# Tile 0's gates, up and output projections first; tile 1's later, during tile 0's search and first expert rows

## What is computed

```python
sh1, sc1, gt1, sh2, sc2, gt2 = split(silu(c) @ w_cond + b_cond)      # adaLN, 12 blocks of 512 columns
h = layernorm(x) * (1 + sc1) + sh1
q, k, v, gu, gv, ga, gg = split(h @ w_in)                            # 9 blocks of 512 columns
attn = causal attention with ALiBi (8 heads of 64)
sgu = gelu(gu) * (lower triangle of w_spatial @ LN(gelu(gv)) + b)    # 8 groups, chunks of 128 tokens
merged = sigmoid(ga) * (attn @ w_attn_up) + sigmoid(gg) * (sgu @ w_gmlp_up)
x = layernorm(ALPHA * x + (1 + gt1) * (merged @ w_out)) * ln1_g + ln1_b
h = layernorm(x) * (1 + sc2) + sh2
for head in range(8):                                                # PEER: 128 x 128 experts
    s = (h @ w_peer_q[head]) against two tables of 128 keys          # two halves of 128
    e, g = the 16 best sums of one key of each half, softmax over them
    p += sum over the 16 of g * gelu(h . peer_u[e]) * peer_v[e]
out = layernorm(ALPHA * x + (1 + gt2) * p) * ln2_g + ln2_b
```

## Time and profile before

| | |
|---|---|
| median of 3 runs | 966.8 us (965.15 to 969.27) |
| span of the profiled execution | 968.9 us |
| TensorE busy | 804.9 us, 83% |
| VectorE busy | 604.0 us, 62% |
| GpSimd busy | 541.7 us, 56% |
| ScalarE busy | 196.0 us, 20% |
| DMA | 338.30 MB, mean 349 GB/s |

### The profile page before, as it was taken

How to read it: one execution, slowest core, us unless ns; L and a number is a source line. 1 busy time by engine, 2 the same in 40 slices (tenths; PEclk the granted TensorE clock), 3 DMA queues, 4 the chain that set the end, 5 groups by cost and what they waited for, 6 DMA issues and landing times.

```text
span 968.9 us, 8991 instructions
## 1 busy us (share of the span) xinstructions
PE 804.9 (83%) x2516; PEld 451.6 (47%) x2516; DVE 604.0 (62%) x1359; ACT 196.0 (20%) x494; POOL 541.7 (56%) x529
## 2 busy tenths in 40 slices
PE   5999999999768687887979787796979688696884
PEld 5877578778424233433334343343334343343331
DVE  6336585225679756576575848557484856687556
ACT  1012122201122312131221213122121213133111
POOL 1000000000478776777777777777777777777772
PEclk9999999999969888989889897997989798898988
DMA  9998974491799999999999999999999999999994
GB/s 348 373 359 315 342 270 174 176 353 37 243 356 350 339 396 372 357 409 366 380 385 392 409 391 410 408 355 386 380 411 351 409 409 354 405 405 379 410 409 196
DMA packets 112267, 338.30 MB, mean 349 GB/s; under 512 B 9184, under 2 KB 20976, under 8 KB 112112
## 3 DMA queue, kind: packets, MB, share of 16 engines
q0 software_dynamic: 73728, 268.47, 71.8%
q1 hardware_dynamic: 35936, 67.11, 19.5%
q10 hardware_dynamic: 2576, 2.37, 0.8%
HBM read 336.87 MB, written 1.05 MB: 349 GB/s over the span
## 4 chain that ended last, share of the span: by engine, by line
PE 46%; POOL 20%; issue 14%; DMA 8%; DVE 7%; ACT 2%; ACTq 2%; DVEq 0%; POOLq 0%
POOL ring L354 20%; PE bank L1142 20%; PE bank L965 9%; DMA ring<-in_peer_u_dram,small 8%; PE bank L1068 3%; PE bank L1082 3%; PE bank L958 3%; DVE ring L811 2%; PE bank L1105 2%; PE bank L914 1%; ACTq L412 1%; PE bank L931 1%; ACT small L510 1%; PE bank L919 1%; DMA x_sb<-in_x_dram 1%
## 5 line engine op out<-in xcount | busy, mean ns | idle before, releaser
L1142 PE MATMUL bank<-ring,small 128*128 128x512 f32 x1012 | 490.0, 646 | 126.3 <-ACT small L510 125.6
L354 POOL DMA_INDIRECT ring<-in_peer_u_dram,small x256 | 269.5, 1053 | 283.8 <-issue 279.2
L811 DVE CUSTOM_DVE_ANT_0 ring<-ring,h_sb 128x1024 f32<-128x1024 f32 x256 | 310.2, 1224 | 185.6 <-DMA ring<-in_peer_u_dram,small 178.5
L1142 PEld LDWEIGHTS bank<-ring,small 128*128 128x128 f32 x1012 | 207.3, 208 | 399.5 <-issue 314.7
L354 POOL DMA_INDIRECT ring<-in_peer_v_dram,small x256 | 268.2, 1047 | 83.2 <-issue 74.5
L965 PE MATMUL bank<-hT,ring 128*128 128x256 f32 x448 | 102.0, 387 | 1.7 <-ACT hT L405 1.1
L965 PEld LDWEIGHTS bank<-hT,ring 128*128 128x128 f32 x448 | 85.8, 194 | 17.0 <-issue 5.4
L510 ACT ACTIVATE small<-ident,small 128x128 f32<-128x128 f32 x253 | 77.4, 388 | 67.6 <-DVE small L802 66.7
L588 DVE SCALAR_TENSOR_TENSOR ln<-ring,c_col,ln 128x512 f32<-128x512 f32 x77 | 57.9, 752 | 2.7
L1105 PE MATMUL bank<-wpq,hT 128*128 (+1 forms) x240 | 54.2, 379 | 0.0
L505 ACT ACTIVATE small<-small 128x8 f32<-128x8 f32 x32 | 6.7, 208 | 222.7 <-DVE small L811 222.7
(11 more groups left out here) (154 smaller groups left out, 491.5 us busy)
## 6 DMA issues: line engine op xcount, KB each, us to landing
ring<-in_w_cond_dram SPq DMA_DIRECT2D x10, 2048.0 KB, 13.8
ring<-in_w_in_dram SPq DMA_DIRECT2D x8, 2048.0 KB, 12.9
wpq<-in_w_peer_q_dram SPq DMA_DIRECT2D x8, 1024.0 KB, 11.9
ring<-in_w_cond_dram SPq DMA_DIRECT2D x4, 1024.0 KB, 14.5
ring<-in_w_out_dram SPq DMA_DIRECT2D x2, 2048.0 KB, 10.7
ring<-in_peer_u_dram,small POOLq DMA_INDIRECT x256, 6.5
ring<-in_peer_v_dram,small POOLq DMA_INDIRECT x256, 6.4
ring<-in_w_in_dram SPq DMA_DIRECT2D x2, 1024.0 KB, 13.3
```

The source lines that it names most:

```text
L354: nc.gpsimd.indirect_dma_start(out=dst[e], out_offset=None, in_=table[0], in_offset=bass.IndirectOffsetOnAxis(ap=idx[:, k:k + 1], axis=0)) ...
L811: V.tensor_tensor_reduce(u_ring[e], u_ring[e], h_sb[:, t, :], 1.0, 0.0, ALU.mult, ALU.add, acol[:, g, e:e + 1]).then_inc(dots_done, 1)
L1142: last = T.matmul(bank[ACC_BANKS[t][m]][:], diag[:, e, :], v_ring[e][:, m * BLK:(m + 1) * BLK], start=False, stop=end, skip_group_check=True)
```

## The change

The gates, the up projections and the output projection are made for one tile at a time.

- `STREAM` now names a slot for each entry. All twelve c blocks come before the first gate block and use slots 2 and 3; input blocks 0 to 4 use slots 0 and 1. The last gate block goes in three parts to `h_sb`, `ln2` and `wpq` (`last_gate`), where nothing else is needed any more. Gate block 5 is loaded a second time later ("again").
- VectorE does `cond_block` 4 to 11 in front of the heads.
- Between the heads TensorE makes the gates of tile 0 alone (`gate_half`, moving operand of 128 columns). The first two gMLP up groups of tile 0 follow the last two heads.
- After the heads: the rest of tile 0's up groups, `project(0)`, whose weights now lie in `wpq` and are loaded when the heads are done, then a gate block and a half of tile 1 (`later`), the transposes of h, query 0, and the other gate blocks, up groups and the merge of tile 1 while the search and the first group's gathers and dot products run. `project(1)` is cut in halves between the rows of pair 0. Tile 1's first norm moves behind pair 2, its modulation behind pair 3.
- w_peer_q: head 1 is loaded before the heads are done, head 0 with the second load of gate block 5, heads 2 to 7 under the gathers.
- The query of pair p+2 is made during pair p, directly transposed (32 instructions of 128 columns in place of 16 of 256, a copy and two transposes).
- All loops are written out; `hold` is gone. GpSimd's waits before u rows are for two dot products at a time.

```diff
-STREAM = [("c", 0), ("c", 1), ("c", 2), ("c", 3), ("in", 0), ("in", 1), ("c", 4), ("in", 2), ("c", 5), ("c", 6),
-          ("in", 3), ("c", 7), ("in", 4), ("c", 8), ("in", 5), ("c", 9), ("in", 6), ("c", 10), ("in", 7), ("c", 11),
-          ("in", 8), ("ua", 0), ("ug", 0), ("o", 0), ("o", 1)]
+STREAM = [("c", 0, 0), ("c", 1, 1), ("c", 2, 2), ("c", 3, 3), ("in", 0, 0), ("in", 1, 1), ("c", 4, 2), ("c", 5, 3),
+          ("in", 2, 0), ("c", 6, 2), ("c", 7, 3), ("in", 3, 1), ("c", 8, 2), ("c", 9, 3), ("in", 4, 0), ("c", 10, 2),
+          ("c", 11, 3), ("in", 5, 1), ("in", 6, 2), ("in", 7, 3), ("ua", 0, 0), ("ug", 0, 1), ("again", 5, 2)]
...
+LATER_GATES = (6, 7, 5, 8)
+FINISH_AT = 12
...
+            sp.wait_ge(attn_ready, HEADS)
+            sp.wait_ge(gate_saved, 2)
+            o_of = w_out[0].rearrange("(k p) n -> p k n", p=P)
+            for m in range(2):
+                sp.dma_start(w_o[m], o_of[:, :, m * BLK:(m + 1) * BLK]).then_inc(o_in[m], 16)
+            sp.wait_ge(merged, KC // 2)
+            head_load(0)
+            block_load("again", 5)
+            sp.wait_ge(later_ready, 4)
+            head_load(2)
+            sp.wait_ge(o_ready, 3)
+            head_load(3)
+            head_load(4)
+            sp.wait_ge(o_ready, 4)
+            head_load(5)
+            head_load(6)
+            head_load(7)
...
+            for n in range(2 * PAIRS):
+                first = n % 4 * GROUP
+                if n % 2 == 0:
+                    pool.wait_ge(idx_ready, n // 2 + 1)
+                for e in range(GROUP):
+                    if n == 0 and e % 4 == 0:
+
+                        pool.wait_ge(later_ready, 2 + e // 4)
+                    elif n and e % 2 == 0:
+                        pool.wait_ge(dots_done, GROUP * (n - 1) + e + 2)
+                    gather(peer_u, u_ring, e, first + e, u_in)
+                for e in range(GROUP):
+                    if n == 0 and e == 0:
+                        pool.wait_ge(gmlp_up_done, 1)
+                    elif n == 0 and e == 4:
+                        pool.wait_ge(up_ready, KC)
+                    elif n and e % 2 == 0:
+                        pool.wait_ge(v_used, GROUP * (n - 1) + e + 2)
+                    gather(peer_v, v_ring, e, first + e, v_in)
...
+            for p in range(PAIRS):
+                dots(2 * p)
+                if p + 1 < PAIRS:
+                    topk_halves(p + 1)
+                weights(2 * p)
+                if p == 0:
+                    dve.wait_ge(later_saved, 4)
+                    merge(1)
+                if p + 1 < PAIRS:
+                    topk_sums(p + 1)
+                if p == 4:
+                    dve.wait_ge(h2_ready, 2 * TILES)
+                dots(2 * p + 1)
+                if p + 1 < PAIRS:
+                    weights(2 * p + 1)
+                if p == 2:
+                    first_norm(1)
+                if p == 3:
+                    modulated(1)
+                if p == FINISH_AT:
+                    dve.wait_ge(ln2_in, 32)
+                    finish(0)
...
+            pe.wait_ge(gate_saved, 2)
+            pe.wait_ge(attn_saved, WC)
+            up_gmlp(0, 2)
+            up_gmlp(0, 3)
             arrived(("ua", 0))
+            for r in range(4):
+                up_attn(0, r)
+            for m in range(2):
+                pe.wait_ge(o_in[m], 16)
+                project(0, m, range(KC))
+            later(0, range(4))
+            later(1, range(2))
             transpose_h(0)
             pe.wait_ge(h2T_saved, 2)
+            query(0)
+            head_scores(0)
+            later(1, range(2, 4))
+            later(2, range(4))
+            pe.wait_ge(later_saved, 2)
+            for r in range(4):
+                last = up_gmlp(1, r)
+            last.then_inc(gmlp_up_done, 1)
+            for r in range(4):
+                up_attn(1, r)
+            query(1)
+            head_scores(1)
+            later(3, range(4))
+            every = tuple(enumerate(range(GROUP)))
+            for p in range(PAIRS):
+                add_rows(2 * p, every)
+                if p + 2 < PAIRS:
+                    query(p + 2)
+                if p == 0:
+                    project(1, 0, range(KC))
+                add_rows(2 * p + 1, every[:3] if p + 1 < PAIRS else tuple(enumerate(PE_ROWS)))
+                if p + 2 < PAIRS:
+                    head_scores(p + 2)
+                if p + 1 < PAIRS:
+                    add_rows(2 * p + 1, every[3:])
+                if p == 0:
+                    project(1, 1, range(KC))
+                if p == 3:
+                    transpose_h(1)
```

More of the change, by code:

```diff
@@ L154, in build @@
         idx = small[:, 2870:2902].bitcast(U32)
[L156 to L161, removed]
+        u_ring = [ring[:, r * D:(r + 1) * D] for r in U_ROWS]
+        v_ring = [ring[:, r * D:(r + 1) * D] for r in V_ROWS]
         def slot(b):
@@ L952, in piece @@
                     arrived(("in", b))
[L953 removed]
+                if n >= 2:
                     pe.wait_ge(piece_saved, n - 1)
@@ L1074, in project @@
-            def project(t):
-                for m in range(2):
-                    arrived(("o", m))
-                    w = slot(("o", m)).rearrange("p (k n) -> p k n", k=KC)
-                    for k in range(KC):
-                        if m == 0 and k % 2 == 0:
-                            pe.wait_ge(merged, KC // 2 * t + k // 2 + 1)
-                        last = T.matmul(bank[OUT_BANKS[t][m]][:], hT[:, k, t * P:(t + 1) * P], w[:, k, :],
-                                        start=(k == 0), stop=(k == KC - 1))
+                if j >= HEADS:
+                    r = j - HEADS
+                    if r == 0:
+                        arrived(("ug", 0))
+                        pe.wait_ge(gate_saved, 2)
+                    pe.wait_ge(half_saved, HEADS - 1 + r)
+                    up_gmlp(0, r)
@@ L1084, in project @@
+            def project(t, m, ks):
+                for k in ks:
+                    if m == 0 and k % 2 == 0:
+                        pe.wait_ge(merged, KC // 2 * t + k // 2 + 1)
+                    last = T.matmul(bank[OUT_BANKS[t][m]][:], hT[:, k, t * P:(t + 1) * P], w_o[m][:, k, :],
+                                    start=(k == 0), stop=(k == KC - 1))
+                if k == KC - 1:
                     last.then_inc(o_ready, 1)
@@ L1149, in _, with add_rows @@
-            zeros = zero_tile[:]
-            arrived(("ua", 0))
-            arrived(("ug", 0))
-            pe.wait_ge(gate_saved, 2)
-            pe.wait_ge(attn_saved, WC - 1)
-            up(0, range(16))
-            project(0)
-            up(1, range(14))
+            def add_rows(n, rows):
+                t = n // (2 * HEADS)
+                for i, e in rows:
+                    pe.wait_ge(v_in[e], 16 * (n + 1))
+                    pe.wait_ge(diag_ready, GROUP * n + i + 1)
+                    first = (n % (2 * HEADS), i) == (0, 0)
+                    end = n % (2 * HEADS) == 2 * HEADS - 1 and e == GROUP - 1
+                    for m in range(2):
+                        last = T.matmul(bank[ACC_BANKS[t][m]][:], diag[:, e, :], v_ring[e][:, m * BLK:(m + 1) * BLK],
+                                        start=first, stop=end, skip_group_check=True)
+                        if end and t == TILES - 1:
+                            last.then_inc(acc_ready, 1)
+                    if not (end and t == TILES - 1):
+                        last.then_inc(v_used, 1)
```

562 lines of the change are left out of this document (265 added, 297 removed).

## The result

The changed kernel takes 951.7 us (median of 8 runs, 948.7 to 955.3) beside 965.3 us for the kernel before on the same chip (8 runs, 957.5 to 969.3): a ratio of 0.988, with a 95% interval of 0.985 to 0.991. 948 was forecast, in a range of 934 to 961. The two profiled executions lie at opposite ends of these runs (968.9 before, 946.9 after), so the 22 us between them are more than the 13.6 between the medians.

| us | before | changed | forecast |
|---|---|---|---|
| to the first gather | 252.96 | 232.71 | 232 |
| pairs 0 to 2 | 140.3 | 148.9 | 142.5 |
| pairs 3 to 15 | 558.4 | 548.0 | 558.4 |
| tail | 17.3 | 17.3 | 17.3 |
| span | 968.9 | 946.9 | 950.4 |

The account below looks back on a forecast made before the run. The prediction took a TensorE stage of 253 us, then 698.6 us of GpSimd gathers lengthened by VectorE, as the bound. 968.9 - 21 (front) + 2.5 (pairs 0 to 2) + 0 = 950.4, or 948 as median; range 934 to 961.

Parts of the forecast that it names:

- The front: Everything up to the first gather: it comes at 232 instead of 252.96 us, -21 us (bounds -9 and -29).
- The gate pieces: TensorE between the heads: eight pieces for tile 0 alone take half of 57.7 us, 28.8 us less.
- the gap with its slow piece: TensorE in the heads: one wait of 3.4 us for the first softmax, plus 2 for the clock.
- front bound by loads and VectorE: Rival before the first gather: blocks take 6.2 us, heads start 8 us later still; 956 us, chance 0.11.
- Pairs 0 to 2: First three pairs of gathers: 142.5 us against 140.2, +2.5 us (bounds -6 and +20).
- the loads: w_peer_q blocks under the first pairs' gathers: six instead of two, four more are 12 us of DMA, 3 taken.
- The waits for TensorE's rows: GpSimd before v rows: waits 5 us in pair 0, 5 in pair 1, none in pair 2.
- the two falls of the clock: First three pairs: TensorE's clock falls twice, costing 3 us.
- The merge: Tile 1's merge on VectorE under gathers: 4.4 us at most, nothing where GpSimd waits for TensorE.
- Pairs 3 to 15: Later gathers: same instructions in the same order, so 0 change from 558.4 us (bounds -19 and +36).
- collisions fall: Rival: VectorE's search gets shorter, dot products follow landings, half of 38.7 us goes; 929 us, chance 0.10.
- The slower case: Rival: dot products start late, run back to back, collisions with gathers grow; 979 us, chance 0.05.

Follow-up runs that it names:

- the last run: Changed kernel with v normalisation, adaLN save and bias broadcast later, query-weight loads spread, last norm's loads after pair 7, pair 0's second search half earlier: 937.9 us, 0.971 times before.
- softmax first and loads spread: Changed kernel with gMLP's v normalisation moved behind the second head's softmax and query-weight loads of heads 4 to 7 issued one at a time: 942.8 us, 0.978 times before.

## Why the prediction held, and where it did not

*The front* (-21): measured -20.3. The gate pieces took 3.84 us, as the row of query 0 that the prediction itself quotes, and not the half of 7.2 that it took, and the gap with its slow piece 7.1 us, not 5.4; the heads ended at 179 and not at 175, the projection at 205.4 and not at 202. That was made good behind the transposes, 16.6 us from there to the first gather instead of 19.2: the first search fell from 10.03 to 8.57 us, and the first gather followed it after 0.29 instead of 1.12 us. So 2.3 of the 20.3 belong to the written-out loops (first gather at 250.66 in the kernel before with its loops written out). Rival "front bound by loads and VectorE" fell; the output weights were covered.

*Pairs 0 to 2* (+2.5): measured +8.6. The mis-sized term is the loads: "four more are 12 us of DMA alone; GpSimd's waits give back most of it, and I take 3". The count was wrong too. The prediction has two of these loads under the gathers in the kernel before; there the last one is issued at 241.92 us and lands 5.4 us later (order of time, then the view of DMA issues from 241 to 300 us: KB, us to landing), ahead of the first gather at 252.96:

```profile
241.92 0.37 SPq L310 DMA_DIRECT2D wpq<-in_w_peer_q_dram  x1
...
wpq<-in_w_peer_q_dram SPq DMA_DIRECT2D x1, 1024.0 KB, 5.4
```

So six loads are new there, 18 us of DMA at the prediction's own rate, and leaving out the six took 14.1 us off these pairs: little was given back. The waits for TensorE's rows were forecast at 10 us in pairs 0 and 1 and were 2.5 there and 5.9 in pair 2; the two falls of the clock did not come in pairs 0 and 1. The merge brought no collisions: the gathers under it take 0.93 to 0.94 us, and none began under one of its four adds. But it stands in front of the second group's dot products: in the last run, with the second half of the search ahead of it and of the weights, pair 0 took 48.8 us, beside 50.8 with softmax first and loads spread.

*Pairs 3 to 15* (0): measured -10.4. The step that failed: "Loops written out spare register work between them; GpSimd's 0.30 us gap shows none to spare, so 0". It looked for the gain on GpSimd. It lay on VectorE: the search took 10.56 to 10.80 us before and takes 8.9 now. A second zero had no good reason either: "q two heads ahead takes a chain of copies off TensorE, which has 104 us of slack" asked what the chain cost TensorE, and it held up VectorE's search by up to 1.8 us. The late start and the search together passed the 10.3 us that there are between two groups of dot products. The rival "collisions fall" had this mechanism, with 19 us of gain; written out alone it gives 16.6 in these pairs of the profiled execution, and the new order takes 6.2 of them back.

*The slower case*, that dot products start late and collisions grow, did not come in the steady pairs, but is what the loads do in pairs 1 and 2: the lengthening there is 13.8 us, and 2.4 without loads.

Open: why the kernel before varies by 12 us between executions, and how much of the 13.6 us in a given run is the search; and how much of the gain in the steady pairs the query two heads ahead would bring by itself. A search between 10.3 and 11.5 us was not tried in the changed kernel.

## What to carry to other kernels

When a change has two parts, an order and a rewriting, time the plain one alone: here it gave as much as both together. The order's 18 us at the front were paid back: 5.6 in pair 0, behind the work that was moved into it, 4.9 in pairs 1 and 2, where loads went under gathers that already filled the queues, and 6.2 after that. A step off the critical path has a budget (here 10.3 us between two groups, for the wait in front of the search and the search together). Within it a shorter step is worth nothing; getting under it was worth 1.8 us a pair (43.13 to 41.32). Ask of a transfer moved under other work whether the queues it goes to are full there.

## What the runs showed of the hardware

A gather that begins in the first 1.0 us of a dot product of VectorE ends about 0.8 us after it, whatever its own start: in the changed kernel 66 of 69 do, and the other three, which begin within 0.03 us of the dot product, take 0.94 us. Of its 512 gathers, by how far into a dot product they began (five of the classes, and those that began with none running):

| us into it | gathers | median us |
|---|---|---|
| 0 to 0.1 | 14 | 1.98 |
| 0.3 to 0.4 | 6 | 1.68 |
| 0.6 to 0.7 | 15 | 1.40 |
| 0.8 to 0.9 | 4 | 1.22 |
| 1.0 to 1.1 | 140 | 0.97 |
| none running | 265 | 0.94 |

One that was already under way when the dot product began was not held up (518.95 above: 0.94 us, with a dot product from 519.43 on; so it was with 29 of 31). The search's multiplications of 128x512 (TENSOR_TENSOR, both operands in SBUF) hold gathers up as well: fourteen began under one and took 1.13 to 1.45 us. But not every VectorE instruction does. Tile 1's merge in pair 0, two rows in order of time:

```profile
262.65 0.68 DVE L750 SCALAR_TENSOR_TENSOR ln<-wpq,bank 128x512 f32<-128x512 f32 x1
...
263.05 0.94 POOL L385 DMA_INDIRECT ring<-in_peer_u_dram,small  x1 [0.31 <-issue]
```

Its first operand is in SBUF, its second in PSUM, and the gather that begins 0.40 us into it takes 0.94 us. The Trainium skill, page "SBUF — State Buffer", section "Who interferes with whom", says that a VectorE instruction with two SBUF inputs contends with a GpSimd one that reads SBUF, and one with at most one SBUF input, outside the two-port performance modes, does not: the trace agrees in both, with 1.98 us under the dot products and 0.94 us under the merge.

Half the bytes made the kernel 4% slower than whole rows (992.2 against 951.7 us): with earlier landings the dot products met the gathers in a worse phase, as the two stretches above show.
